# In the first attention stage the next head's first scores stand ahead of the second half of its projection piece 4; pieces are issued in halves

## The reference

```
q1, q2, k1, k2, v = projections of rms_norm(h)       # 2 x 64 wide queries and keys, values 128 wide
q, k = rotary(q), rotary(k)                          # on the first 16 of 64 dims
a = softmax(mask(q1 k1^T / 8)) - lam * softmax(mask(q2 k2^T / 8))
o = rms_norm(a v, g_sub) * (1 - lam_init)            # then h + concat(o) @ w_o
```

## Time and profile before

| | us |
|---|---|
| median of 3 runs | 2238.44 |
| lowest, highest | 2237.21, 2238.57 |
| profiled execution | 2242.87 |
| its span, first to last instruction | 2240.8 |
| TensorE busy | 2167.4 (97%) |
| VectorE busy | 1139.5 (51%) |
| GpSimd busy | 1108.4 (49%) |
| ScalarE busy | 786.5 (35%) |
| mean granted TensorE clock | 0.99 of full speed |

### The profile page before, as it was taken

One profiled execution on the slowest core, in us unless ns is written; L12 is line 12 of the kernel. 1 busy time (PEld: TensorE's weight loads), 2 busy tenths in 40 slices (PEclk: granted clock), 3 DMA queues, 4 the chain that ended last, 5 costly groups with the idle time before them and its releaser, 6 DMA issues.

```text
span 2240.8 us, 40385 instructions
## 1 busy us (share of the span) xinstructions
PE 2167.4 (97%) x14044; PEld 1900.3 (85%) x14044; DVE 1139.5 (51%) x2068; ACT 786.5 (35%) x1407; POOL 1108.4 (49%) x1384
## 2 busy tenths in 40 slices
PE   8999899999999899999999999999999999999997
PEld 7888699999999776669999999977778878888886
DVE  6666735334146777763443514775631364425244
ACT  3434524222133355542432222433433224323232
POOL 4444236545556411114655555664545675646554
PEclk9999999999999999989999999999999999999999
DMA  4212122222223101102232222322222232222322
GB/s 171 75 68 66 57 76 94 95 85 94 94 76 113 66 30 38 37 29 80 85 103 85 94 94 85 104 81 79 85 82 98 94 113 94 98 90 94 103 85 75
DMA packets 52502, 188.25 MB, mean 84 GB/s; under 512 B 5824, under 2 KB 5952, under 8 KB 52416
## 3 DMA queue, kind: packets, MB, share of 16 engines
q1 hardware_dynamic: 51408, 185.16, 24.0%
q10 hardware_dynamic: 1008, 1.89, 0.3%
HBM read 184.93 MB, written 2.10 MB: 83 GB/s over the span
## 4 chain that ended last, share of the span: by engine, by line
PE 89%; DVE 7%; ACT 2%; issue 2%; DMA 0%; DVEq 0%; SPq 0%; ACTq 0%
PE ps L451 26%; PE ps L452 26%; PE ps L453 26%; PE ps L573 3%; PE ps L610 2%; PE ps L612 1%; PE ps L592 1%; DVE g_lo L817 1%; DVE g_hi L815 1%; DVE scratch L935 1%; PE ps L764 1%; ACT scratch L1468 1%; PE ps L596 1%; DVE scratch L1016 0%; ACT scratch L1524 0%
## 5 line engine op out<-in xcount | busy, mean ns | idle before, releaser
L433 POOL TENSOR_TENSOR w_lo<-w_raw,w_hi 128x256 fp32r<-128x256 f32 x1380 | 1108.2, 835 | 1107.9 <-ACT w_hi L1378 1107.9
L451 PE MATMUL ps<-x_hi,w_hi 128*128 128x264 f32 (+2 forms) x2760 | 880.2, 319 | 3.7 <-DVE scratch L1343 2.4
L452 PE MATMUL ps<-x_lo,w_hi 128*128 128x264 f32 (+2 forms) x2760 | 867.2, 314 | 0.0
L453 PE MATMUL ps<-x_hi,w_lo 128*128 128x264 f32 (+2 forms) x2760 | 866.4, 314 | 0.0
L451 PEld LDWEIGHTS ps<-x_hi,w_hi 128*128 128x128 f32 x2760 | 520.5, 189 | 49.0 <-issue 7.7
L452 PEld LDWEIGHTS ps<-x_lo,w_hi 128*128 128x128 f32 x2760 | 520.3, 189 | 33.4 <-issue 0.8
L453 PEld LDWEIGHTS ps<-x_hi,w_lo 128*128 128x128 f32 x2760 | 520.1, 188 | 32.4
L1378 ACT ACTIVATE w_hi<-w_raw 128x1024 fp32r<-128x1024 f32 x345 | 361.4, 1051 | 315.8 <-PE ps L453 313.1
L451 PE MATMUL ps<-g_hi,w_hi 128*128 128x264 f32 (+2 forms) x1312 | 409.9, 312 | 15.4 <-DVE g_lo L817 14.6
L452 PE MATMUL ps<-g_lo,w_hi 128*128 128x264 f32 (+2 forms) x1312 | 408.6, 311 | 0.0
L453 PE MATMUL ps<-g_hi,w_lo 128*128 128x264 f32 (+2 forms) x1312 | 407.8, 311 | 0.0
(11 more groups left out here) (166 smaller groups left out, 1749.8 us busy)
## 6 DMA issues: line engine op xcount, KB each, us to landing
w_raw<-stream SPq DMA_DIRECT2D x345, 512.0 KB, 3.2
h<-x_t SPq DMA_DIRECT2D x4, 528.0 KB, 8.7
out_t<-h SPq DMA_DIRECT2D x8, 256.0 KB, 2.1
scratch<-rotary_tables ACTq DMA_DIRECT2D x4, 264.0 KB, 5.6
par<-params ACTq DMA_DIRECT2D x1, 342.5 KB, 5.2
scratch<-positions ACTq DMA_DIRECT2D x1, 256.0 KB, 2.6
cst<-shape_constants ACTq DMA_DIRECT2D x1, 193.0 KB, 6.6
```

The lines of the kernel that those rows point to most:

```text
L433: last = nc.gpsimd.tensor_tensor(w_lo[:, j % 4, cols], w_raw[:, j % 4, cols], w_hi[:, j % 4, cols].bitcast(F32), ALU.subtract)
L451: nc.tensor.matmul(out_ap, w_hi[:, s, c], xh[:, k, cols], start=first, stop=False)
L452: nc.tensor.matmul(out_ap, w_hi[:, s, c], xl[:, k, cols], start=False, stop=False)
L453: return nc.tensor.matmul(out_ap, w_lo[:, s, c], xh[:, k, cols], start=False, stop=last)
```

## The change

TensorE's body gets a new order, and `piece_a` can be issued in halves (`part` 0: the first four k, 12 matmuls; `part` 1: the last four, with the signal that the piece is done). The body is now: first half of N's piece 0, transposes 0, its second half, values 0; scores 2, transposes 1, N's piece 1, values 1; scores 3, transposes 2, N's piece 2, values 2; scores 4, transposes 3, N's piece 3, values 3, transposes 4; first half of N's piece 4; N's scores 0; second half of piece 4; values 4; N's piece 5; N's scores 1; N's value transposes. Scores 1 of a head thus stand at the end of the body before (for head 0, behind its value transposes). On DVE N's maximum 0 goes ahead of the take of piece 4, and output 4 ahead of the take of piece 5. ACT, GpSimd and SP have the lists of before. Nothing is computed that was not computed before.

```diff
--- before.py
+++ after.py
@@ -506,11 +506,12 @@
                 if k == KD - 1:
                     last.then_inc(ss_ready, 1)
 
-            def piece_a(hd, p):
+            def piece_a(hd, p, part=None):
 
                 m, c = divmod(p, 2)
-                wait(pe, chunk_taken, 6 * hd + p - 1)
-                for k in range(KD):
+                if part != 1:
+                    wait(pe, chunk_taken, 6 * hd + p - 1)
+                for k in range(4 if part == 1 else 0, 4 if part == 0 else KD):
                     b = KD * m + k
                     if not c and (k == 0 or b % 6 == 0):
                         pe.wait_ge(lo_ready, J_A + 4 * hd + b // 6 + 1)
@@ -522,7 +523,7 @@
                         first_sum(k + 3)
                     if c and (b % 6 == 5):
                         last.then_inc(half_done, 1)
-                if p < 5:
+                if p < 5 and part != 0:
                     last.then_inc(chunk_done, 1)
 
             def piece_b(hd, s, p):
@@ -641,23 +642,35 @@
                 def step(f, idx):
                     f("A", hd, par_, idx)
 
-                def piece(p):
-                    if more:
-                        piece_a(hd + 1, p)
-                    elif p != 4:
-                        sub_sum(min(p, 4), 0)
-                for idx in range(5):
-                    if idx < 4:
-                        step(scores, idx + 1)
-                    elif more:
-                        scores("A", hd + 1, 1 - par_, 0)
-                    step(transposes, idx)
-                    piece((0, 1, 2, 3, 5)[idx])
-                    step(values, idx)
-                    if idx == 3:
-                        piece(4)
-                if more:
-                    value_transposes("A", hd + 1, 1 - par_)
+                if not more:
+                    for idx in range(5):
+                        if idx and idx < 4:
+                            step(scores, idx + 1)
+                        step(transposes, idx)
+                        sub_sum(idx, 0)
+                        step(values, idx)
+                    return
+                nxt = hd + 1
+                piece_a(nxt, 0, 0)
+                step(transposes, 0)
+                piece_a(nxt, 0, 1)
+                step(values, 0)
+                step(scores, 2), step(transposes, 1)
+                piece_a(nxt, 1)
+                step(values, 1)
+                step(scores, 3), step(transposes, 2)
+                piece_a(nxt, 2)
+                step(values, 2)
+                step(scores, 4), step(transposes, 3)
+                piece_a(nxt, 3)
+                step(values, 3), step(transposes, 4)
+                piece_a(nxt, 4, 0)
+                scores("A", nxt, 1 - par_, 0)
+                piece_a(nxt, 4, 1)
+                step(values, 4)
+                piece_a(nxt, 5)
+                scores("A", nxt, 1 - par_, 1)
+                value_transposes("A", nxt, 1 - par_)
 
             def head_b(hd, turn, s, first=False, more=True):
 
@@ -694,6 +707,7 @@
                 piece_a(0, p)
             scores("A", 0, 0, 0)
             value_transposes("A", 0, 0)
+            scores("A", 0, 0, 1)
             head_a(0, 0)
             with pe.Fori(0, (HEADS_A - 2) // 2) as i:
                 for n in range(2):
@@ -1045,11 +1059,11 @@
                     nxt(piece_a, idx)
                     take_output("A", hd, par_, idx, hd)
                 sub_norm_of(3)
-                nxt(piece_a, 4)
                 if more:
                     maximum("A", hd + 1, 1 - par_, 0)
+                nxt(piece_a, 4)
+                take_output("A", hd, par_, 4, hd)
                 nxt(piece_a, 5)
-                take_output("A", hd, par_, 4, hd)
                 if more:
                     combine("A", hd + 1, 1 - par_, 0)
                 sub_norm_of(4)
```

## The result

The changed kernel takes 2245.36 us in the median of 17 runs (2242.74 to 2254.4), the kernel before 2238.66 in 17 runs beside them (2236.81 to 2244.22). The ratio is 1.0029, with a 95% interval of 1.0019 to 1.0039: slower by 6.7 us (the interval is 4.3 to 8.7), where the forecast was 6.2, to 2244.6 us. One run of one kernel of the experiments (values(4) behind piece 5 again) took 3567.34 us at a mean granted clock of 0.61 and is left out of that kernel's numbers.

The account below looks back on a forecast made before the run. TensorE, 89% of the span, was taken as the bound; two waits go, two come. Six periods at +0.82, +1.37 and -0.10 give +6.2 us, put on the median: 2244.6 us; range +0.6 to +8.5 us.

Parts of the forecast that it names:

- The waits that go: TensorE's waits at a head's first transposes for combine (0.48 us) and value transposes for the last output copy (0.47) vanish.
- The first new wait: The next head's first scores wait on TensorE for DVE's rotated queries: 0.84 us a period.
- release: Time from the end of the awaited instruction to TensorE's start; taken as 0.15 us, bounds 0 and 0.24.
- The second new wait: values(0) on TensorE wait for ACT's copy of the transposed probabilities: 0.63 us a period.
- The chain from the take of piece 5 to L1494: Take of piece 5, combine(0), maximum(1), exponentials of scores(1), ACT's copy: 5.63 us without the output copy.
- starts off the same steps: GpSimd's work still starts off the same steps of pieces 3 and 5, so the change does not part it from DVE's instructions.
- The sum: Six periods at +0.82 us, +1.37 in head 6, -0.10 in the last head: +6.2 us.
- the 1.37: DVE's take of piece 5 comes 1.37 us later behind piece 3: 12.76 us instead of 11.39.
- No change: Rival: the new stall moves GpSimd's low parts out of DVE's way; +1.2 us, 2239.6 us; chance 0.22.
- Faster, nothing takes the waits' place: Rival: the two old waits go and no new ones come; -3.5 us, 2235 us; chance 0.06 with its neighbourhood.
- The clock falls: Rival: granted clock falls once a period for 3 us at half speed; +10 us on top, 2255 us; chance 0.04.
- The price of a new run of matmuls: Cutting a piece in two on TensorE costs 0.09 us for each new run, 0.09 of the 1.37.

Follow-up runs that it names:

- the experiment: The changed kernel with values(4) behind piece 5 again on TensorE and its output copy behind the take of piece 5 on DVE; ratio 1.0024 to the kernel before.
- combine first: The changed kernel with the next head's combine(0) ahead of the take of piece 5 on DVE; ratio 0.9990 to the kernel before.
- the two mends: The changed kernel with the third high part behind the next head's first exponentials and combine(0) ahead of the take of piece 5; ratio 0.9986 to the kernel before.

## Why the prediction was right

**The waits that go.** Both went, as worked out; neither L593 on L1030 nor L631 on L1037 waits in a period any more.

**The first new wait.** Forecast: arrival at 5.43 us behind piece 3, ready at 6.12, release 0.15, wait 0.84. Measured: arrival 5.47, ready 6.10, release 0.13, wait 0.76. The way on to the take of piece 5 was 6.49 and is 132.91 - 126.43 = 6.48. The slack of a step, less what is taken away in front of it, gave the wait to 0.08 us.

**The second new wait.** Forecast 0.63, measured 0.88. The chain from the take of piece 5 to L1494 was put at 5.63 us and is 138.75 - 132.91 = 5.84. The term that was mis-sized is L1028: the sum kept its 0.49, and it takes 0.75. The release was 0.05 where 0.15 was put, and TensorE was ready earlier than forecast, 5.01 us behind the take instead of 5.15. So the wait is off by 0.21 - 0.10 + 0.14 = 0.25, but the period by 0.12 only: 12.71 us from piece 3 to the take (12.76 forecast), 5.89 on to values(0) (5.78), 11.96 on to the next piece 3 (11.90). The 17.91 us that the prediction gives for values(0) before is a slip, it is 11.39 + 6.33 = 17.72; nothing was worked out from it.

The prediction said that GpSimd's work "starts off the same steps", and for the last low part this is where it was off. It starts off ACT's high part, which follows the exponentials of the next head. These end at 130.95 now, 1.96 us ahead of the take of piece 5, where before they ended with that take. So the low part began at 132.05, ahead of combine, and L1028 met it. The Trainium skill (SBUF — State Buffer, Who interferes with whom) has the pair of ports that VectorE and GpSimd share as a lock: when a VectorE instruction runs in a two-port mode, which it says `tensor_scalar` can enter, whoever issues first has the pair for the whole instruction and the other waits in full. This case's traces agree: 1.07 beside 2.98, or 0.49 beside 3.55, and the ends give the lock away. (Which of the two issued first they do not tell: in the experiment L1028 loses although the profile has it start 0.05 us ahead.) From 30 to 272 us in all eleven traces L1028 (or the same instruction at another line) was stretched 40 times, to between 0.66 and 1.08 us, and each time it ended 0.29 or 0.30 us behind the end of a GpSimd instruction. The 0.75 is such a meeting in the middle of a GpSimd instruction: 134.16 + 0.29 - 133.70 = 0.75.

The instructions with two inputs of 528 columns do the same. L949, L951 and L1030 and their like were stretched 206 times, and each time they ended 0.56 or 0.57 us behind a GpSimd instruction; L951 is 1.13 us long in place of 0.71 because it waits, not because it runs slower. In the other direction, a GpSimd instruction that was held up ended 0.58 to 0.60 us behind the end of the VectorE instruction. So the time of L1028 could have been forecast from the two starts, and its time in the old trace could not be carried over.

**The sum.** Counted from scores to scores, the forecast is -0.6 ahead of head 1, six periods at +0.82, and +1.9 behind the first scores of head 7 (the 1.37 and the 0.59 by which the scores come earlier behind piece 3, less 0.10). Measured are -0.6, six times +0.96 and +2.0: +7.2 in the trace where 6.2 were forecast, and the medians have +6.7. The mechanism, both places and the sign were right; the size was 1.0 us low in the trace and 0.5 in the medians.

**The rivals.** *No change* needed the low parts out of the way. Nothing moved them away; one even came nearer. But its pricing held: moving one low part gave 0.50 us a period, against 0.42 for L951 alone, which is all that the rival counted, and 0.51 with L949. *Faster, nothing takes the waits' place*, needed 0.69 us of slack that was not there. *The clock falls* is not seen in the periods (1.00 from 66 to 243 us in both traces). The 17 runs of the changed kernel have a mean granted clock of 0.992 in the median, and the 66 runs of the kernel before in the experiments are at 0.991 and 0.992.

**The cuts.** The price of a new run of matmuls was put at 0.09 us. One row bears on it: 127.72 to 129.37, 1.65 us for the half piece with the step to values, where 1.60 was forecast.

## What to carry to other kernels

Before a step is put earlier on the busiest engine, subtract what it loses in front of it from its slack: 0.74 us of slack less half a piece of 1.46 was a new wait of 0.76 us, most of the 0.95 that the change removed, and everything behind it waits too. Look for a mend at the engine that is late before the busiest engine's list is given another order: one DVE step put ahead of another and one low part moved took the period from 30.56 to 28.92 us with TensorE's list untouched, as good as giving back part of that list (29.15, and 28.82 with a low part moved as well). Where two engines share a path, the new order also moves their meetings, so a duration of the old trace cannot be carried over where one of them met the other or may meet it now: L1028 went from 0.49 to 0.75 and 1.07.

## What the runs showed of the hardware

**Two engines, one at a time.** A single-input DVE instruction of 528 columns in SBUF took 0.49 us alone, and anything from 0.66 to 1.08 beside GpSimd's 256-column subtractions, which take 0.73 alone. In one kernel it was bistable from period to period, with GpSimd taking the other half of the loss (2.98 or 3.55 us for the same four instructions). A two-input one of 528 columns took 0.71 us alone (up to 1.13 beside GpSimd) or 0.77 alone (up to 1.24), by its kind. Each stretched one ended a fixed time behind the GpSimd instruction that it met, 0.29 us (one input) or 0.57 us (two inputs): in these traces they take turns and do not share.

**The spread of the times goes with the clock.** Seventeen runs of one kernel spread over 7 to 12 us. Each run of the changed kernel and of the experiments has its mean granted clock on record, and within each kernel the time follows it closely: 2242.74 us at 0.995, 2254.4 at 0.987, with a correlation of -0.97 over the 17 runs of the changed kernel (-0.85 to -0.99 in the others) and 0.8 us left around a straight line of 1.4 us per 0.001. The lines of the kernel before (31 and 35 runs) have 1.5 us per 0.001. Read at 0.992, the changed kernel is at 2246.4 us and the kernel before at 2239.5 and 2239.7: +6.8, between the +6.7 of the medians and the +7.2 of the trace. Read so, piece 4 whole is +2.1, combine first +0.2 and the two mends -3.8; their output projections start 2.1 later, 0.3 later and 3.4 us earlier than before. The two traces of the changed kernel show one piece of that spread: the stretch at the lower granted clock in head 7, worth 2.3 us, which only one of them has, behind waits that are the same up to there.

**Small groups of matmuls.** The value transposes took 0.67 us behind a wait and ahead of scores, and 0.52 without a wait and ahead of a piece. Which of the two differences it is was not tested.
